# Expert gate and up weights loaded as two 2 MiB transfers, and the order of products that goes with it

## What is computed

```python
def expert_block(args):
    xb, e = args
    return (jax.nn.silu(xb @ w1[e]) * (xb @ w3[e])) @ w2[e]
```

## Time and profile before

| | us |
|---|---|
| median of 3 runs | 1833.98 |
| lowest and highest | 1831.85, 1839.39 |
| the profiled execution | 1832.78 |
| its span | 1831.0 |
| TensorE busy in it | 1678.4 |
| matmuls of L2711 (gate and up, large blocks), 544 | 239.6 |
| matmuls of L2722 (gate and up, small blocks), 480 | 106.5 |
| matmuls of L2741 (down, large blocks), 272 | 119.6 |
| matmuls of L2738 (down, small blocks), 240 | 54.8 |

### The profile page before, as it was taken

How to read it: one execution, slowest core, us unless ns; L and a number is a source line. 1 busy time by engine, 2 the same in 40 slices (tenths; PEclk the granted TensorE clock), 3 DMA queues, 4 the chain that set the end, 5 groups by cost and what they waited for, 6 DMA issues and landing times. The chain is left out here.

```text
span 1831.0 us, 28314 instructions
## 1 busy us (share of the span) xinstructions
PE 1678.4 (92%) x11406; PEld 1148.7 (63%) x11406; DVE 711.0 (39%) x1110; ACT 501.6 (27%) x931; POOL 349.1 (19%) x656
## 2 busy tenths in 40 slices
PE   5999999899989986998899999469999999999986
PEld 5688888887878864777778788334444444444432
DVE  4655455430117766777564555530000000000005
ACT  1641111122117753554431322101111111111112
POOL 1100011200010005677520011101111111111115
PEclk9999999999989988988889999679999999999997
DMA  9358756531426712312535122465999999999986
GB/s 331 122 200 297 244 204 230 172 126 45 115 79 152 171 37 62 75 42 57 165 122 196 50 103 104 202 231 198 390 401 393 395 400 388 393 401 387 397 350 264
DMA packets 150796, 397.92 MB, mean 217 GB/s; under 512 B 49371, under 2 KB 65786, under 8 KB 127264
## 3 DMA queue, kind: packets, MB, share of 16 engines
q1 hardware_dynamic: 121120, 328.77, 49.9%
q0 software_dynamic: 14816, 41.33, 6.3%
q10 hardware_dynamic: 14752, 26.29, 3.8%
HBM read 338.86 MB, written 66.40 MB: 221 GB/s over the span
## 5 line engine op out<-in xcount | busy, mean ns | idle before, releaser
L2711 PE MATMUL psum<-w,ex_x_t 128*128 128x512 f32 x544 | 239.6, 599 | 5.4 <-DMA w<-in_exp_w 4.3
L2711 PEld LDWEIGHTS psum<-w,ex_x_t 128*128 128x128 f32 x544 | 102.7, 191 | 131.9 <-issue 123.1
L2856 DVE TENSOR_TENSOR ex_sigm<-psum,ex_sigm 128x512 f32<-128x512 f32 x17 | 11.8, 691 | 360.4 <-ACT ex_sigm L2819 360.4
L558 ACT ACTIVATE stage<-psum 128x512 f32<-128x512 f32 (+1 forms) x72 | 41.3, 574 | 299.4 <-PE psum L160 180.3
L158 PE MATMUL psum<-w_even,h_hi 128*128 128x512 f32 (+1 forms) x320 | 118.7, 371 | 4.7 <-ACT stage L558 4.7
L2741 PE MATMUL psum<-w,ex_hid_t 128*128 128x512 f32 x272 | 119.6, 593 | 0.0
L160 PE MATMUL psum<-w_even,h_lo 128*128 128x512 f32 (+1 forms) x320 | 118.4, 370 | 0.0
L159 PE MATMUL psum<-w_even,h_hi 128*128 128x512 f32 (+1 forms) x320 | 118.4, 370 | 0.0
L2722 PE MATMUL psum<-w,ex_x_s 128*64 128x512 f32 x480 | 106.5, 595 | 0.9 <-DMA w<-in_exp_w 0.9
L2819 ACT ACTIVATE ex_sigm<-psum 128x512 f32<-128x512 f32 (+1 forms) x32 | 16.0, 499 | 321.3 <-PE psum L2711 224.2
L158 PE MATMUL psum<-w_odd,h_hi 128*128 128x512 f32 x256 | 100.0, 391 | 0.0
(11 more groups left out here) (470 smaller groups left out, 3493.7 us busy)
## 6 DMA issues: line engine op xcount, KB each, us to landing
w<-in_exp_w SPq DMA_DIRECT2D x128, 1024.0 KB, 15.8
w<-in_exp_w SPq DMA_DIRECT2D x32, 2048.0 KB, 10.8
w_ring<-in_ada_w SPq DMA_DIRECT2D x12, 2048.0 KB, 11.2
w_ring<-in_w_in SPq DMA_DIRECT2D x10, 2048.0 KB, 10.3
qk<-stage_r ACTq DMA_DIRECT2D x16, 512.0 KB, 7.5
gates<-stage ACTq DMA_DIRECT2D x32, 256.0 KB, 2.0
bl_gates<-gates SPq DMA_DIRECT2D x8, 1024.0 KB, 4.8
w<-pair_rows SPq DMA_DIRECT2D x16, 512.0 KB, 10.0
```

The source lines that it names most:

```text
L558: nc.scalar.activation(stage[:, b, 0:n], ps[:, 0:n], ACT.Sigmoid if kind == "gate" else ACT.Copy).then_inc(sig("proj_evac"), 1)
L2711: last = nc.tensor.matmul(bank[2 + j], x_t[:, par, k, :], w13[:, par, j, k, :], start=(k == 0), stop=(k == KT - 1))
L2856: nc.vector.tensor_tensor(sigm[:], bank[2], sigm[:], ALU.mult).then_inc(sig(f"silu{par}"), 1)
```

## The change

`load_up` now loads one whole matrix, j = 0 for gate or j = 1 for up: one transfer of 2 MiB, 16 KB a partition, with a semaphore of its own. `up_big` does the eight products of the gate and then the eight of up; it waits for gate's transfer before the first and for up's before the ninth. `up_small`, whose products need both matrices at every k, waits for both transfers before its first product and raises `up_used` by two at its end. `load_next` is the same text, with q now read as the matrix.

```diff
-HALF_K = KT // 2
-
-def load_up(nc, sp, sig, keep, ins, par, q, e):
-
-    for j, name in enumerate(("exp_w1", "exp_w3")):
-        w = ins[name][0]
-        src = w[e] if isinstance(e, int) else w[bass.ds(e, 1)].rearrange("a k n -> (a k) n")
-        src = src.rearrange("(p k) n -> p k n", k=KT)[:, q * HALF_K:(q + 1) * HALF_K, :]
-        sp.dma_start(keep["w13"][:, par, j, q * HALF_K:(q + 1) * HALF_K, :], src).then_inc(sig(f"w13_in{par}{q}"), 16)
+def load_up(nc, sp, sig, keep, ins, par, j, e):
+
+    w = ins[("exp_w1", "exp_w3")[j]][0]
+    src = w[e] if isinstance(e, int) else w[bass.ds(e, 1)].rearrange("a k n -> (a k) n")
+    sp.dma_start(keep["w13"][:, par, j], src.rearrange("(p k) n -> p k n", k=KT)).then_inc(sig(f"w13_in{par}{j}"), 16)
 ...
             def up_big(blk):
                 par, pair = blk
+                for j in range(2):
+                    pe.wait_ge(sig(f"w13_in{par}{j}"), 16 * (pair + 1))
+                    for k in range(KT):
+                        last = nc.tensor.matmul(bank[2 + j], x_t[:, par, k, :], w13[:, par, j, k, :], start=(k == 0), stop=(k == KT - 1))
+                    last.then_inc(sig(f"up_used{par}"), 1)
+
+            def up_small(blk):
+
+                par, pair = blk
+                for j in range(2):
+                    pe.wait_ge(sig(f"w13_in{par}{j}"), 16 * (pair + 1))
                 for k in range(KT):
-                    if k % HALF_K == 0:
-                        pe.wait_ge(sig(f"w13_in{par}{k // HALF_K}"), 32 * (pair + 1))
-                    for j in range(2):
-                        last = nc.tensor.matmul(bank[2 + j], x_t[:, par, k, :], w13[:, par, j, k, :], start=(k == 0), stop=(k == KT - 1))
-                    if k % HALF_K == HALF_K - 1:
-                        last.then_inc(sig(f"up_used{par}"), 1)
-
-            def up_small(blk):
-
-                par, pair = blk
-                for k in range(KT):
-                    if k % HALF_K == 0:
-                        pe.wait_ge(sig(f"w13_in{par}{k // HALF_K}"), 32 * (pair + 1))
                     for h in range(2):
                         last = nc.tensor.matmul(bank[5][h * SMALL:(h + 1) * SMALL, :].rearrange("p (j n) -> p j n", j=2), x_s[:, k, :],
                                                 w13[:, par, :, k, h * FE // 2:(h + 1) * FE // 2], start=(k == 0), stop=(k == KT - 1))
-                    if k % HALF_K == HALF_K - 1:
-                        last.then_inc(sig(f"up_used{par}"), 1)
+                last.then_inc(sig(f"up_used{par}"), 2)
```

## The result

| | us |
|---|---|
| before, median of 4 runs | 1832.91 |
| changed, median of 4 runs | 1860.3 (1856.07 to 1866.81) |
| ratio | 1.0146, 95% interval 1.0106 to 1.0186 |
| changed, the profiled execution | 1866.81, span 1864.8 |

On another chip, beside other runs of the kernel before, the changed kernel took 1852.98 us, a ratio of 1.0127 (1.0052 to 1.0202). So the change costs 1.3 to 1.5%. The forecast was 1840.5 in a range of 1832 to 1851: slower was right as to the sign of the sum, the size was not.

The account below looks back on a forecast made before the run. TensorE and the transfers were both taken to be at their limit. Waits of 4.2 + 12 x 0.68 = 12.4 us instead of 4.6 added 7.8 to 1832.78, giving 1840.5 us, range 1832 to 1851.

Parts of the forecast that it names:

- What bounds the kernel: Expert stage: TensorE and DMA both at their limit, 34.4 us a pair; no slack at the small block's start.
- The floor: TensorE's least time for a pair of blocks, 34.15 us; removing all waits could save at best 4.6 us.
- Part 1, the large block's order: Large block, gate then up: equal bytes needed at each point, successive products into one bank free; cost 0.
- Part 2, SyncE's issues: Two 2 MiB transfers for four of 1 MiB in every burst: the saved issuing is hidden, 0 us.
- Part 3, the pieces: Gate and up weights in 16 KB pieces a partition: -0.2 us a burst, two bursts 34.0 us.
- Part 4, first occurrence: Small block at 1310.27 must wait for all its weights to land: a wait of 4.2 us.
- Part 4, steady pairs: Later small blocks wait 0.68 us each, 12 times, as the queue briefly runs dry; period 34.83 us.
- the row of an empty queue: Burst issued at 1275.13 into an empty queue: 1.0 us of work in 2.87 us, so 1.9 us lost.
- w: TensorE's wait before a small block, from period = 34.0 + 1.5 - w = 34.15 + w: 0.68 us.
- The burst doesn't shorten: Rival: weights land 20.9 us after issue whatever is left queued; waits 23.2 us, +18.6, 1851 us; chance 0.20.
- Cover holds: Rival: enough engines still work at the next burst's issue, so later small-block waits vanish; 1833 us, chance 0.19.
- transfers no limit: Rival: three-transfer bursts land before any product asks, so all 4.6 us of waits go; 1828 us, chance 0.05.

Follow-up runs that it names:

- the wait alone: The kernel before, with only the small block waiting for both halves of its gate and up weights ahead of its first product: 1847.35 us, ratio 1.0090.
- the new order of issues: SyncE issues gate and up loads as their buffers come free; kernel before 1825.27 us, changed kernel 1827.56, changed kernel with small block by matrix 1824.14.
- the second profile: The changed kernel run again without further edits, on another chip: median 1852.98 us, ratio 1.0127, profiled execution 1850.51 us.
- no gathers: The changed kernel with the loop's indirect gathers bounded to row 0, so nearly no token rows are moved: one execution, 1835.79 us.

## Why the prediction failed, by its own steps

- **What bounds the kernel: half right.** That TensorE and the transfers are both at their limit, and that no slack stands before the second half of the small block's weights, is what the run with the wait alone shows, and the waits at the end of the kernel with the new order of issues show the transfers' side once more. The floor was not one: 34.15 us a pair came from two pairs without a transfer in the chain, and TensorE does a pair in 33.91 us with the loads issued earlier. The pieces of a chain don't begin where a block does: by the starts of the products (1671.98, 1706.11, 1740.12) the same two pairs took 34.13 and 34.01.
- **Part 1, the large block's order: right.** In the changed kernel large blocks wait 0.5 us in all. Products in succession into one bank cost nothing: 238.3 us busy after, 239.6 before.
- **Part 2, SyncE's issues: right** that fewer issues save nothing. It passed over the order of these issues, which turned out to be worth more than anything else here.
- **Part 3, the pieces: right for the weights, incomplete for the rest.** Two bursts back to back pass in 34.4 to 34.6 us with 8 KB pieces and in 34.2 to 35.0 with 16 KB (twice 17.1 to 17.5, where enough was left); a gain of 0.4 isn't seen. What the step left out is who else uses the queue: it said that gathers "move along" and gave them no price. They land 4 us later beside 16 KB pieces, and one wait of 4.0 to 4.7 us came of it in all four kernels that had the pieces and the old order of issues.
- **Part 4, first occurrence: right.** 4.2 us forecast, 4.4 measured (3.2 in the second profile).
- **Part 4, steady pairs: the step that failed.** The mechanism is the one forecast; the term mis-sized is the time lost when a burst is issued with little left in the queue. I took 1.9 us from the row of an empty queue. From landing to landing it is 2.8 us, the mean of seven bursts (2.3 to 3.4). Two smaller terms went the same way: the two bursts take 34.5 us and not 34.0, as nothing came of the larger pieces, and TensorE's pair is 33.91 and not 34.15. With these three the same equation gives w = (34.5 + 2.8 - 0.37 - 33.91)/2 = 1.5 us, and 4.2 + 12 x 1.5 = 22 us of waits, against 19.2 to 23.6 measured; the 2.8 alone gives w = 1.1 and 18 us. The row did not show the tail. I took the last landing of a burst for its end, and part of the engines are idle before that: DMA shares of the kernel before at a small down product's end (1380.01) were

```profile
1378.00:1379.00 1.00, 1.00 (x8) 0.35 (x6) 0.00 (x0) 0.00 (x0) 0.00 (x0) 1.00 0.99 410
1379.00:1380.00 1.00, 1.00 (x7) 0.19 (x4) 0.00 (x0) 0.00 (x0) 0.00 (x0) 1.00 0.85 352
1380.00:1381.00 1.00, 1.00 (x8) 0.55 (x10) 0.00 (x0) 0.99 (x2) 0.18 (x1) 1.00 0.61 254
1381.00:1382.00 1.00, 1.00 (x8) 0.40 (x6) 0.00 (x0) 0.19 (x1) 0.42 (x2) 1.00 0.78 287
```

  although X landed only at 1383.7. The cover of 3.7 us was less than it looked, but not yet used up: up to 1.3 us could be taken from it at no loss, as eleven of the twelve bursts with 2.4 us or more left show. Below that what is missing is lost. After, with 0.7 us left at the issue of 1417.01:

```profile
1416.00:1417.00 1.00, 1.00 (x5) 0.47 (x4) 0.00 (x0) 0.00 (x0) 0.00 (x0) 1.00 0.47 197
1417.00:1418.00 1.00, 1.00 (x5) 0.52 (x4) 0.00 (x0) 0.90 (x1) 0.00 (x0) 1.00 0.19 33
```

  That the share dips because the 16 engines end a burst at different times fits these rows, but which engine ends when was not measured.
- **What had no term.** The wait for gathered rows (3.7 us) and the clock (5.5 us in the first profile) were put at nothing: gathers and stores "move along", and a fall of the clock isn't mentioned. Together they are more than the whole forecast of 7.8.
- **The rivals.** "The burst doesn't shorten" came nearest in size, and I gave it 0.20. Two measured values of issue to landing, 20.9 and 21.2 us from very different queues, spoke for it. Its own sign, large blocks over 35.5 us apart, was seen (35.7), but that sign doesn't tell it from a restart cost of 2.8 us; the bursts with 2.4 to 2.9 us left do, and they are against it. So its number was near by luck in part: its 20.9 us is too long and its floor of 34.15 too. Its wait before a small block was given as 1.6 us; the mean of the later twelve is (23.6 - 4.4)/12 = 1.6. "Cover holds", "transfers no limit" and the Trainium skill's fixed cost for each DMA ("DMA: Bandwidth & Descriptors", section Anatomy of one DMA) all pointed the other way; taking two of five transfers out of a burst freed nothing, as 17.2 us for a burst of five and 17.1 to 17.5 for one of three show. (In that section the Trainium skill fits its figure to transfers that GpSimd issues; the weights are issued by SyncE.)
- **The sum.** The waits for weights made +18.9 us in the first profile where I had +7.8; beyond them came 3.7 for the gathered rows and 5.5 for the clock. Neither had a place in my range, which ended at the rival's 1851.

## What to carry to other kernels

Before asking for a transfer earlier in a computation, look for when it is issued, not only when it lands: here one wait on the issuing engine, standing ahead of loads whose buffers had long been free, made the difference between -0.4% and +1.3%. Where loads go out in bursts, the time from last landing to last landing holds only while enough of the burst before is left: compare many bursts with their issues, at different fillings of the queue, and read the DMA share around the next issue for how much cover there is. When an earlier issue helps, follow the time to landing of one load from pair to pair; if it grows, the kernel is living on a lead. And give every other user of the queue, small gathers too, a price when the pieces beside them grow.

## What the runs showed of the hardware

- **Clock.** The granted clock fell to the lower level behind waits of 4.44 and 2.31 us (8.75 us for small products instead of 7.09), but not behind one of 2.85 us at 1545.14: 1.00 from 1545 to 1549. In other kernels it stayed up behind a wait of 3.28 us (the wait alone, at 1306.45) and fell behind one of 2.01 (no gathers, at 1316.45: 0.57 from 1317 to 1321). The length of a wait alone doesn't tell it. The third line is that of the 3.28 us.

```profile
1326.00:1332.00 6.00, 5.18 (x13) 1.71 (x15) 0.00 (x0) 0.00 (x0) 0.62 (x1) 0.50 1.05 397
...
1545.00:1549.00 4.00, 3.86 (x18) 1.61 (x20) 0.00 (x0) 0.00 (x0) 1.00 (x2) 1.00 1.01 413
...
1306.00:1310.00 4.00, 3.55 (x18) 1.53 (x20) 0.00 (x0) 0.00 (x0) 1.00 (x1) 1.00 1.01 386
```

- **Gathers beside larger pieces.** Indirect gathers land after 13.0 to 16.2 us beside 16 KB pieces and after 9.9 to 12.1 beside 8 KB, with the same rows to move. The bytes of the rows aren't the reason: with nearly all rows out of bounds the gathers of 128 still land after 13.8 to 15.2 us beside 16 KB pieces. What is was not tried apart.
- **A queue that runs dry.** A burst of 6 MiB in three transfers lands 17.1 to 17.5 us after the one before if 2.4 us or more of that one are left at its issue (eleven of twelve bursts), and 19.5 to 20.6 us after its own issue if 1.4 us or less are left (seven). In five transfers, with 3.7 us or more left, it is 17.0 to 17.4 (the kernel before, bursts issued from 1309 to 1672 us).
- **Scatter of stages nobody touched.** The start of the first block lies between 1204.5 and 1227.4 us in ten profiles, so a difference of some us in one execution's span must be looked up in its stage first.
